# A routing matrix built in groups of four tokens: 36 blocks of the first expert table computed between the groups, and the weighted one-hots handed to GpSimd

## The chip, the core and the metric

The kernel runs on one core of a Trainium2 chip. Its engines are TensorE (PE in the profile; its weight loads are PEld), VectorE (DVE), ScalarE (ACT), GpSimd (POOL) and SyncE (SP), which here only issues DMAs. The metric is the device time of one execution in microseconds (us), as the median of several runs. Before the change it is 1849.74 us (three runs, 1848.17 to 1851.37 us).

## What is computed

The reference is a two-layer chain on 256 tokens of width 1024. The change touches one part of it, the PEER layer (product keys into a table of 16384 experts):

```python
q = (t @ w_q).reshape(n_tok, PEER_HEADS, 2, PEER_HALF)
sc = jnp.einsum("thpk,hpnk->thpn", q, sub_keys)
s_top, i_top = lax.top_k(sc, 16)                    # per head and half
...                                                 # 16 x 16 sums, best 16 of them
idx = i_top[..., 0] * 128 + i_top[..., 1]           # expert = (i, j)
g = jax.nn.softmax(best, axis=-1)
act = gelu(einsum("phkd,pd->phk", u_tab[idx], t))
out = einsum("phk,phkd->pd", g * act, v_tab[idx])
```

The kernel does not gather experts. It computes every expert for every token: block j of `u_tab` holds the 128 experts (i, j), so `gelu(u_block_j @ t)` is a tile of 128 experts by 256 tokens. It is multiplied by the routing matrix W[i, j, token], which is zero but where the token chose the expert, and the product is multiplied by block j of `v_tab`. There are 128 blocks in each table, 512 KB each.

## The kernel before

Work on fp32 operands goes in two forms. In the first, a 128 x 1024 piece of weights is loaded to a slot of a ring of four (`raw`), ACT copies it to fp32r (`high`, `take_high`), and DVE makes the rest (`low` = raw - high, `take_low`); TensorE then takes three products of the halves. `project_in` (L944 to L946) is 8 x 3 matmuls with 256 columns and makes a block of u; `project_out` (L963 to L967) is 12 matmuls with 512 columns and adds a block of v to banks 0 to 3. In the second form ("native", L1028) the fp32 operands are used as they are.

The PEER layer has four stages, one behind the other.

1. Selection. In four rounds TensorE makes queries and scores, DVE takes the top sixteen of each (the longest chain here), and TensorE fills its time with 24 native blocks of u (`EARLY_OF_ROUND` = 4, 4, 4, 12), the last 24 blocks of the table. ACT leaves their gelu in `arena`, where the routing matrix will lie.
2. TensorE computes block 0 of u, turns the selected weights, i and j to tokens-in-columns (`sel_turned`, L1039), ACT copies them to `chosen`, TensorE computes blocks 1 and 2.
3. The routing matrix, 64 groups of four tokens. For each token one matmul of two 128 x 128 one-hot tiles gives W[:, :, token] (L1054): the one-hot of i (DVE, one 128 x 512 instruction for the group, L1563), and the one-hot of j times the weight. The latter is made by DVE for 2.5 of four tokens (L1567) and by ACT for 1.5 (two instructions each, L735 and L743). ACT copies columns 0 to 103 to `arena` (L754), DVE multiplies the last 24 into the gelus that lie there (L1557). No blocks are computed, and no DMA runs, because a ring slot holds `chosen` and SP waits in `expert_step(0)` until all one-hots are there.
4. The expert loop, 128 steps. Step j is `project_out` of block j of v and, as long as j + 3 < LATE = 104, `project_in` of block j + 3 of u. Steps 0 to 100 have both, 101 to 127 have only v.

GpSimd takes some inverse roots of variances (`tensor_tensor` with pow on a 128 x 1 tile, L551) and is idle otherwise. The order on each engine is as written, and an engine works through its instructions in that order, held by semaphores. In stage 3 a group has two sets of one-hot tiles in turn (`n % 2`): a new one waits for `scat_done` of the group two back.

Of the kernel before, what the change touches and what calls it, by code (L numbers as in the profile page):

```python
# [44 lines left out]
PARTS = 128  # L45
# [23 lines left out]
EARLY = sum(EARLY_OF_ROUND)  # L69
LATE = NKEYS - EARLY  # L70

# [38 lines left out]
STREAM = [("mix", 8 * KC), ("mix_out", KC), ("query", 16), ("expert", NKEYS + LATE),  # L110
# [50 lines left out]

def piece_u(j, it=0):

    return Piece("expert", j if j < 3 else 2 * j - 2, it, 8)
# [21 lines left out]
def build(nc, x, w_mix, w_gate, w_out, w_query, keys, u_tab, v_tab, diff_qk, diff_v, diff_out,  # L186
# [3 lines left out]
    with ctx:  # L190
# [17 lines left out]
        ffn_params = sb("ffn_params", [PARTS, 2 * FF_CHUNKS * 4])  # L208
        subln = sb("subln", [PARTS, PARTS])
        stats = sb("stats", [PARTS, 64])  # L210
# [20 lines left out]
        def weights_of(token, j, j_end):  # L231

            return arena[:, :].rearrange("p (j t) -> p j t", t=SEQ)[:, j:j_end, bass.ds(token, 4)].rearrange("p j t -> p t j")
# [5 lines left out]
        def act_tokens(g):  # L239

            return (3,) if g % 2 == 0 else (2, 3)

        def scattered(g):

            return bank(g).rearrange("p (t j) -> p t j", t=4)
# [16 lines left out]
        chosen = raw[:, 2 * D:2 * D + 3 * SEQ]  # L262
        minus_weight = raw[:, 2 * D + 3 * SEQ:3 * D]
        distance = [ps[:, 7 * HALF + PARTS * n:7 * HALF + PARTS * (n + 1)] for n in range(4)]
# [96 lines left out]
        one_hots_ready, act_one_hots_ready = sem("one_hots_ready"), sem("act_one_hots_ready")  # L361
        distance_ready, scat_done, w_written = sem("distance_ready"), sem("scat_done"), sem("w_written")
# [82 lines left out]
        def _(sp):  # L445
# [21 lines left out]
            sp.dma_start(ffn_params[:, :], ffn_params_in).then_inc(ffn_params_loaded, 16)  # L467
# [5 lines left out]
            for it, early in enumerate(EARLY_OF_ROUND):  # L473
                for q in range(4 * it, 4 * it + 4):
                    load(Piece("query", q), w_query[q])
                if it == 3:
                    for j in range(3):
                        load(piece_u(j), u_tab[j])
                if it == 0:

                    sp.wait_ge(merged_ready, KC)
                for p in range(p, p + early):
                    if p >= 4:
                        sp.wait_ge(early_done, p - 3)
                    sp.dma_start(early_u[p % 4], u_tab[LATE + p]).then_inc(early_loaded[p % 4], 16)
                p += 1
                if it == 0:

                    sp.wait_ge(h_ready, TB)
                    sp.dma_start(h_saved, h_tok[:, :]).then_inc(h_kept, 16)  # L490
            def expert_step(j, it):
                if j == NKEYS - 2:

                    sp.wait_ge(coef_low, LATE)
# [7 lines left out]
                if opening(it) and j == 0:  # L502

                    sp.wait_ge(one_hots_ready, SEQ // 4)
                    sp.wait_ge(act_one_hots_ready, SEQ // 4)
# [37 lines left out]
        def _(pool):  # L543
# [10 lines left out]
            inverse_roots(0, 3)  # L554
# [13 lines left out]
        def _(a):  # L568
# [49 lines left out]
            a.activation(stats[:, 60:61], stats[:, 61:62], ACT.Square)  # L618
# [77 lines left out]
            for it in range(4):  # L696
                for q in range(4):
# [5 lines left out]
                    if 4 * it + q < 15:  # L703
                        ahead(p)
# [7 lines left out]
                for early in range(early, early + EARLY_OF_ROUND[it]):  # L712
                    if early == EARLY - 4:

                        a.wait_ge(shifted_ready, 1)
                        a.activation(sel[:, 0:SEQ], sel[:, 0:SEQ], ACT.Exp).then_inc(exp_ready, 1)
                    a.wait_ge(early_done, early + 1)
                    a.activation(part((LATE + early) * SEQ, SEQ), bank(4 + early % 4, 0, SEQ), ACT.Gelu_apprx_tanh
                                 ).then_inc(early_gelu, 1)
                early += 1  # L720
            v0, u0 = piece_v(0), piece_u(0)
            take_high(v0)
            ahead(u0)
            for b in range(2):
                a.wait_ge(sel_turned, b + 1)
                n = (2 - b) * SEQ
                a.activation(chosen[:, b * HALF:b * HALF + n], bank(b, 0, n), ACT.Copy).then_inc(chosen_ready, 1)

            a.activation(minus_weight, bank(0, 0, SEQ), ACT.Copy, scale=-1.0).then_inc(chosen_ready, 1)
            a.wait_ge(chosen_ready, 3)  # L730

            def distances(token, g):

                for u in act_tokens(g):
                    ins = a.activation(distance[2 * (g % 2) + u - 2], iota, ACT.Abs, scale=-1.0,  # L735
                                       bias=at(chosen, token + (2 * SEQ + u), 1))
                ins.then_inc(distance_ready, 1)

            def act_one_hots(token, g, n):

                a.wait_ge(distance_ready, n)
                for u in act_tokens(g):
                    ins = a.activation(one_hot_w[g % 2][:, u * PARTS:(u + 1) * PARTS], distance[2 * (g % 2) + u - 2], ACT.Relu,  # L743
                                       scale=at(minus_weight, token + u, 1), bias=at(chosen, token + u, 1))
                ins.then_inc(act_one_hots_ready, 1)

            def scatter_round(it, last=False):
                for g in range(4):  # L750
                    if not (last and g >= 2):
                        distances(it * 16 + (4 * g + 8), g)
                    a.wait_ge(scat_done, it * 4 + (g + 1))
                    a.activation(weights_of(it * 16 + 4 * g, 0, LATE), scattered(g)[:, :, 0:LATE], ACT.Copy).then_inc(w_written, 1)  # L754
                    if not (last and g >= 2):
                        act_one_hots(it * 16 + (4 * g + 8), g, it * 4 + (g + 3))

            a.wait_ge(h_kept, 16)
            for g in range(2):
                distances(4 * g, g)  # L760
                act_one_hots(4 * g, g, g + 1)
            with a.Fori(0, SEQ // 16 - 1) as it:
                scatter_round(it)
            scatter_round(SEQ // 16 - 1, last=True)


# [28 lines left out]
            a.wait_ge(scat_done, SEQ // 4)  # L795
            gelu_block(0, first=True)
            gelu_block(1, first=True)
# [131 lines left out]
        def _(pe):  # L929
# [103 lines left out]

            pe.wait_ge(early_gelu, EARLY)
            project_in(piece_u(0), bank(4, 0, SEQ))
# [7 lines left out]
            for j in (1, 2):  # L1043
                project_in(piece_u(j), bank(4 + j, 0, SEQ))


            def scatter_round(it):
                for g in range(4):
                    pe.wait_ge(one_hots_ready, it * 4 + (g + 1))
                    pe.wait_ge(act_one_hots_ready, it * 4 + (g + 1))  # L1050
                    if not opening(it):
                        pe.wait_ge(early_weighed, it * 4 + (g - 3))
                    for u in range(4):
                        ins = pe.matmul(bank(g, u * PARTS, PARTS), one_hot[g % 2][:, u * PARTS:(u + 1) * PARTS],  # L1054
                                        one_hot_w[g % 2][:, u * PARTS:(u + 1) * PARTS], start=True, stop=True)
                    ins.then_inc(scat_done, 1)

# [861 lines left out]
```

## Time and profile before

| | |
|---|---|
| median of 3 runs | 1849.74 us |
| profiled execution: its span (the page gives no other time of it) | 1851.6 us |
| stage 3, from the first to the last group | about 374.6 to 477.1 us |
| expert loop, from the first matmul of v | from 479.74 us |
| busy: PE, DVE, ACT, POOL | 93%, 68%, 50%, 1% |

The span is from the first to the last instruction. A busy PE is not PE at its peak, since matmuls are pipelined and their ends are modelled: the distance from one start to the next says what one costs. The same holds for ACT and DVE where rows overlap.

### The profile page before, as it was taken

Reading aid. Unit: us, or ns where it says so; the run is one execution under the profiler, and the core shown is the slowest. Engines: PE = TensorE matmul, PEld = TensorE weight load, DVE = VectorE, ACT = ScalarE, POOL = GpSimd, SP = SyncE. Lnnn points to the kernel's source line nnn. Section 1 sums busy time; section 2 is a strip of 40 time slices with the busy share of each in tenths; the row PEclk is TensorE's granted clock in tenths of the full one; section 3 lists DMA queues with packets and bytes.
Section 4 is the critical chain, followed back from the end, with each engine's and each line's share of the span. In section 5 each row is a group of like instructions: output and inputs, shape, how many; then the busy total and the mean of one; then the engine's idle time right before and its main releaser. Section 6 shows DMA issues by size and latency. Waiting matters only on the chain.

```text
span 1851.6 us, 32033 instructions
## 1 busy us (share of the span) xinstructions
PE 1724.4 (93%) x11238; PEld 1567.2 (85%) x11238; DVE 1260.4 (68%) x2341; ACT 925.5 (50%) x1554; POOL 21.9 (1%) x29
## 2 busy tenths in 40 slices
PE   7999799977899999999999998886999989989997
PEld 7999699865799999999999886765999968779997
DVE  6888689999655555555555565685767675566766
ACT  5666533299644444444444454544444444544443
POOL 0000000000000000000000000001000000000000
PEclk9999899999999999999999998998999989999999
DMA  6556634300455555555555565322555544245552
GB/s 198 174 189 201 204 119 144 114 0 0 149 191 182 191 183 190 183 188 186 189 185 187 187 219 175 115 93 90 193 183 191 182 137 126 80 137 186 188 182 102
DMA packets 81305, 292.19 MB, mean 158 GB/s; under 512 B 9056, under 2 KB 10848, under 8 KB 80864
## 3 DMA queue, kind: packets, MB, share of 16 engines
q1 hardware_dynamic: 79632, 286.00, 45.9%
q10 hardware_dynamic: 1616, 5.45, 0.9%
q8 instruction: 34, 0.56, 0.1%
q14 instruction: 23, 0.19, 0.0%
HBM read 289.31 MB, written 2.10 MB: 157 GB/s over the span
## 4 chain that ended last, share of the span: by engine, by line
PE 75%; DVE 10%; issue 9%; ACT 5%; ACTq 1%; POOL 0%; DMA 0%; SPq 0%; DVEq 0%; POOLq 0%
PE ps L944 14%; PE ps L946 14%; PE ps L945 14%; PE ps L963 10%; PE ps L965 10%; PE ps L967 10%; DVE low L1230 1%; ACT h_tok L743 1%; ACT ps L735 1%; ACT arena L754 1%; PE ps L1102 1%; PE ps L939 1%; DVE arena L1529 1%; DVE arena L1531 1%; DVE h_tok L1297 1%
## 5 line engine op out<-in xcount | busy, mean ns | idle before, releaser
L1230 DVE TENSOR_TENSOR low<-raw,high 128x1024 fp32r<-128x1024 f32 (+1 forms) x517 | 623.1, 1211 | 438.8 <-ACT high L595 425.6
L595 ACT ACTIVATE high<-raw 128x1024 fp32r<-128x1024 f32 (+1 forms) x517 | 540.9, 1049 | 621.8 <-PE ps L946 335.5
L944 PE MATMUL ps<-xh,low 128*128 128x256 f32 x2376 | 680.8, 287 | 13.7 <-DVE xl L1251 7.6
L945 PE MATMUL ps<-xl,high 128*128 128x256 f32 x2376 | 675.1, 284 | 0.0
L946 PE MATMUL ps<-xh,high 128*128 128x256 f32 x2376 | 675.0, 284 | 0.0
L944 PEld LDWEIGHTS ps<-xh,low 128*128 128x128 f32 x2376 | 458.7, 193 | 24.4 <-DVE xl L1251 8.2
L945 PEld LDWEIGHTS ps<-xl,high 128*128 128x128 f32 x2376 | 458.7, 193 | 7.4 <-issue 1.7
L946 PEld LDWEIGHTS ps<-xh,high 128*128 128x128 f32 x2376 | 458.3, 193 | 0.0
L963 PE MATMUL ps<-high,yl 128*128 128x512 f32 x688 | 215.2, 394 | 2.8 <-issue 2.6
L965 PE MATMUL ps<-low,yh 128*128 128x512 f32 x688 | 213.8, 392 | 0.0
L967 PE MATMUL ps<-high,yh 128*128 128x512 f32 x688 | 213.3, 391 | 0.0
L965 PEld LDWEIGHTS ps<-low,yh 128*128 128x128 f32 x688 | 129.8, 189 | 28.7
L967 PEld LDWEIGHTS ps<-high,yh 128*128 128x128 f32 x688 | 129.7, 189 | 28.2
L963 PEld LDWEIGHTS ps<-high,yl 128*128 128x128 f32 x688 | 120.3, 190 | 20.0 <-issue 2.8
L1054 PE MATMUL ps<-h_tok 128*128 128x128 f32 x512 | 73.1, 286 | 29.6 <-DVE h_tok L1567 17.0
L1054 PEld LDWEIGHTS ps<-h_tok 128*128 128x128 f32 x512 | 61.9, 191 | 40.7 <-issue 14.6
L1028 PE MATMUL ps<-arena 128*128 128x256 f32 x384 | 83.5, 379 | 0.0
L1028 PEld LDWEIGHTS ps<-arena 128*128 128x128 f32 x384 | 72.7, 190 | 9.7
L754 ACT ACTIVATE arena<-ps 128x416 f32 (+1 forms) x64 | 71.8, 1122 | 3.7 <-PE ps L1054 3.7
L963 PE MATMUL ps<-high,xl 128*128 128x512 f32 x160 | 53.3, 416 | 9.5 <-DVE xl L1240 4.2
L743 ACT ACTIVATE h_tok<-ps,raw 128x128 f32<-128x128 f32 x96 | 53.3, 668 | 0.1
L965 PE MATMUL ps<-low,xh 128*128 128x512 f32 x160 | 51.7, 405 | 0.0
(215 smaller groups left out, 1479.4 us busy)
## 6 DMA issues: line engine op xcount, KB each, us to landing
raw<-in_v_tab SPq DMA_DIRECT2D x128, 512.0 KB, 3.3
raw<-in_u_tab SPq DMA_DIRECT2D x104, 512.0 KB, 3.2
raw<-in_ffn_in SPq DMA_DIRECT2D x88, 512.0 KB, 3.2
raw<-in_w_mix SPq DMA_DIRECT2D x56, 512.0 KB, 4.4
raw<-in_ffn_out SPq DMA_DIRECT2D x44, 512.0 KB, 3.3
arena<-in_u_tab SPq DMA_DIRECT2D x24, 512.0 KB, 3.4
raw<-in_w_query SPq DMA_DIRECT2D x16, 512.0 KB, 5.8
raw<-in_diff_qk SPq DMA_DIRECT2D x16, 512.0 KB, 3.4
```

The source lines that it names most:

```text
L595: a.activation(cols(high, p, 0, n), cols(raw, p, 0, n), ACT.Copy).then_inc(slot_high[p.slot], 1)
L743: ins = a.activation(one_hot_w[g % 2][:, u * PARTS:(u + 1) * PARTS], distance[2 * (g % 2) + u - 2], ACT.Relu, scale=at(minus_weight, token ...
L754: a.activation(weights_of(it * 16 + 4 * g, 0, LATE), scattered(g)[:, :, 0:LATE], ACT.Copy).then_inc(w_written, 1)
L944: pe.matmul(dst, left[1], right[0], start=start, stop=False)
L945: pe.matmul(dst, left[0], right[1], start=False, stop=False)
L946: return pe.matmul(dst, left[0], right[0], start=False, stop=stop)
L963: pe.matmul(bank(2 * t + half), src_low[:, xs], cols(high, p, half * HALF, HALF), start=first, stop=False)
L965: pe.matmul(bank(2 * t + half), src_high[:, xs], cols(low, p, half * HALF, HALF), start=False, stop=False)
L967: ins = pe.matmul(bank(2 * t + half), src_high[:, xs], cols(high, p, half * HALF, HALF), start=False, stop=last)
L1028: ins = pe.matmul(bank(4 + early % 4, 0, SEQ), early_u[early % 4][:, k * PARTS:(k + 1) * PARTS], chunk_of(xf, k), start=(k == 0), stop=(k ...
L1054: ins = pe.matmul(bank(g, u * PARTS, PARTS), one_hot[g % 2][:, u * PARTS:(u + 1) * PARTS], one_hot_w[g % 2][:, u * PARTS:(u + 1) * PARTS], ...
L1230: v.tensor_tensor(cols(low, p, 0, n), cols(raw, p, 0, n), cols(high, p, 0, n).bitcast(F32), ALU.subtract).then_inc(slot_low[p.slot], 1)
```

## The change

- Of the 104 blocks of u that came behind the selection, 36 are now "staged": blocks 103 down to 68 (`staged_block(k)` = 103 - k). Four (LEAD) are computed after the native ones, before the selection is turned. The other 32 stand between the groups of the routing matrix, one behind each second group, in PSUM banks 4 to 7 in turn. LATE falls from 104 to 68.
- A staged block that is computed behind group n holds tokens of which the weights are already known. ACT writes the gelu of those in place in PSUM, and DVE multiplies them into `arena`; the gelu of the other tokens goes to `arena`, and is weighed by the group's own multiplication, which grows from 24 columns to 28 and then by one for each second group, up to 59. ACT's copy shrinks by the same.
- The one-hot of j times the weight is made by GpSimd for all tokens, one `tensor_scalar` (is_equal, mult) on 128 x 128 each, 256 in all. DVE's 160 and ACT's 2 x 96 instructions for it are gone.
- Weights, i and j move from the ring slot to `spare` and `yh`, so the ring goes on through stage 3 and SP's wait is gone. Blocks 0, 1 and 2 of u are computed behind the last group. ACT's exp of the scores moves from the middle of the last native blocks to behind them. The loops over groups are written out.

```diff
+LEAD, STAGED = 4, 36
+FIRST_NATIVE = NKEYS - NATIVE
+EARLY = NATIVE + STAGED
 LATE = NKEYS - EARLY
+def first_staged(n):
+    return FIRST_NATIVE - LEAD - n // 2
...
+        weight = spare[:, :]
+        sel_i, sel_j = (yh[:, SEQ * n:SEQ * n + SEQ].bitcast(F32) for n in range(2))
...  (GpSimd)
+            pool.wait_ge(chosen_ready, 3)
+            pool.wait_ge(h_kept, 16)
+            for n in range(GROUPS):
+                if n >= 2:
+                    pool.wait_ge(scat_done, n - 1)
+                for u in range(4):
+                    t = 4 * n + u
+                    ins = pool.tensor_scalar(one_hot_w[n % 2][:, u * PARTS:(u + 1) * PARTS], iota, sel_j[:, t:t + 1], weight[:, t:t + 1],
+                                             ALU.is_equal, ALU.mult)
+                ins.then_inc(j_hots_ready, 1)
...  (ScalarE)
+            for k in range(LEAD):
+                p = piece_staged(k)
+                a.wait_ge(slot_done[p.slot], p.count)
+                a.activation(staged_part(k, 0, SEQ), staged_bank(k, 0, SEQ), ACT.Gelu_apprx_tanh).then_inc(staged_ready, 1)
+                ahead(p)
+            a.wait_ge(sel_turned, 1)
+            a.activation(yh[:, 0:SEQ], bank(0, SEQ, SEQ), ACT.Copy).then_inc(chosen_ready, 1)
...
+            for n in range(GROUPS):
+                a.wait_ge(scat_done, n + 1)
+                j_end = first_staged(n)
+                a.activation(weights_of(n, 0, j_end), scattered(n)[:, :, 0:j_end], ACT.Copy).then_inc(w_written, 1)
+                if n % 2 == 1:
+                    k, t = LEAD + n // 2, 4 * (n + 1)
+                    p = piece_staged(k)
+                    if n > 1:
+                        ahead(p.later(-1))
+                    a.wait_ge(slot_done[p.slot], p.count)
+                    ins = a.activation(staged_bank(k, 0, t), staged_bank(k, 0, t), ACT.Gelu_apprx_tanh)
+                    if t < SEQ:
+                        ins = a.activation(staged_part(k, t, SEQ), staged_bank(k, t, SEQ), ACT.Gelu_apprx_tanh)
+                    ins.then_inc(staged_ready, 1)
...  (TensorE)
-            project_in(piece_u(0), bank(4, 0, SEQ))
+            for k in range(LEAD):
+                project_in(piece_staged(k), bank(4 + k % 4, 0, SEQ))
...
+            for n in range(GROUPS):
+                pe.wait_ge(i_hots_ready, n + 1)
+                pe.wait_ge(j_hots_ready, n + 1)
+                if n >= 4:
+                    pe.wait_ge(early_weighed, n - 3)
+                for u in range(4):
+                    ins = pe.matmul(bank(n % 4, u * PARTS, PARTS), one_hot[n % 2][:, u * PARTS:(u + 1) * PARTS],
+                                    one_hot_w[n % 2][:, u * PARTS:(u + 1) * PARTS], start=True, stop=True)
+                ins.then_inc(scat_done, 1)
+                if n % 2 == 1:
+                    k = LEAD + n // 2
+                    pe.wait_ge(staged_ready, LEAD)
+                    if k >= 2 * LEAD:
+                        pe.wait_ge(staged_weighed, k - 2 * LEAD + 1)
+                    project_in(piece_staged(k), bank(4 + k % 4, 0, SEQ))
+            for j in range(3):
+                pe.wait_ge(staged_weighed, STAGED - LEAD - 3 + j)
                 project_in(piece_u(j), bank(4 + j, 0, SEQ))
...  (VectorE)
-                for q in range(4 * it, min(4 * it + 4, 15)):
+                for q in range(4 * it, 4 * it + 4):
                     ahead(Piece("query", q))
...
+            for n in range(0, GROUPS, 2):
+                k = LEAD + n // 2
+                if n + 2 < GROUPS:
+                    v.wait_ge(scat_done, n + 1)
+                    i_hots(n + 2)
+                if n >= 2:
+                    weigh_staged(k - 1)
+                if n + 3 < GROUPS:
+                    v.wait_ge(scat_done, n + 2)
+                    i_hots(n + 3)
+                weigh_group(n)
+                weigh_group(n + 1)
+                take_low(piece_staged(k).later(1))
```

On TensorE, the start of the routing matrix before: the turns are L1039, block 1 and 2 of u stand between them and the first group, and the groups (L1054, four matmuls each) stand back to back.

```order
L1039 MATMUL ps<-consts,arena 128x128 [waits sel_ready]
L1039 MATMUL ps<-consts,arena 128x128 x5
...
L1054 MATMUL ps<-h_tok 128x128 [waits act_one_hots_ready,one_hots_ready]
L1054 MATMUL ps<-h_tok 128x128 x3
L1054 MATMUL ps<-h_tok 128x128 [waits act_one_hots_ready,one_hots_ready]
```

The same place now (turns L1058, groups L1069, `project_in` L962 to L964):

```order
L1058 MATMUL ps<-consts,arena 128x128 x5
L1069 MATMUL ps<-h_tok 128x128 [waits j_hots_ready,i_hots_ready]
L1069 MATMUL ps<-h_tok 128x128 x3
L1069 MATMUL ps<-h_tok 128x128 [waits j_hots_ready,i_hots_ready]
L1069 MATMUL ps<-h_tok 128x128 x3
...
L964 MATMUL ps<-xh,high 128x256
L1069 MATMUL ps<-h_tok 128x128 [waits j_hots_ready,i_hots_ready]
```

Behind each second group stand the 24 matmuls of a block. Four blocks stand ahead of the turns, where there was one, and none between the turns and the first group.

On VectorE, two groups before (L1563 the one-hots of i, L1567 those of j with the weight, L1557 the multiplication of the native blocks):

```order
L1563 TENSOR_TENSOR h_tok<-raw,consts 128x512 [waits scat_done]
L1567 TENSOR_SCALAR h_tok<-consts,raw 128x128 x3
L1557 TENSOR_TENSOR arena<-arena,ps 128x4x24 [waits w_written]
L1563 TENSOR_TENSOR h_tok<-raw,consts 128x512 [waits scat_done]
L1567 TENSOR_SCALAR h_tok<-consts,raw 128x128 x2
L1557 TENSOR_TENSOR arena<-arena,ps 128x4x24 [waits w_written]
```

And two groups now (L1578 the one-hots of i, L1592 a staged block's known tokens, L1586 the multiplication of the groups, L1255 the low half of a piece of the ring):

```order
L1578 TENSOR_TENSOR h_tok<-yh,consts 128x512 [waits scat_done]
L1592 TENSOR_TENSOR arena<-arena,ps 128x8 [waits staged_ready]
L1578 TENSOR_TENSOR h_tok<-yh,consts 128x512 [waits scat_done]
L1586 TENSOR_TENSOR arena<-arena,ps 128x4x29 [waits w_written] x2
L1255 TENSOR_TENSOR low<-raw,high 128x1024 [waits slot_high2]
```

The five `tensor_scalar` are gone; a low half of 1024 columns and the staged multiplication are new. On GpSimd, the first two groups and the third:

```order
L577 TENSOR_TENSOR stats<-stats 128x1 [waits var_ready] x3
L589 TENSOR_SCALAR h_tok<-consts,yh,spare 128x128 [waits h_kept,chosen_ready]
L589 TENSOR_SCALAR h_tok<-consts,yh,spare 128x128 x7
L589 TENSOR_SCALAR h_tok<-consts,yh,spare 128x128 [waits scat_done]
L589 TENSOR_SCALAR h_tok<-consts,yh,spare 128x128 x3
```

Before, nothing stood here but the inverse roots. Every group's four instructions now wait for the group two back.

## Rows read from the trace of the kernel before

**Rows 1.** The page: busy time of the engines.
```profile
PE 1724.4 (93%) x11238; PEld 1567.2 (85%) x11238; DVE 1260.4 (68%) x2341; ACT 925.5 (50%) x1554; POOL 21.9 (1%) x29
```

**Rows 2.** Busy time by stretch; the first row names the columns.
```profile
core 0: us, PE busy (x) PEld busy (x) DVE busy (x) ACT busy (x) POOL busy (x), PEclk, DMA share, GB/s
374.40:477.20 102.80, 73.14 (x514) 61.83 (x513) 96.96 (x280) 101.07 (x249) 0.00 (x0) 1.00 0.00 0
479.70:485.00 5.30, 5.26 (x13) 4.13 (x14) 3.06 (x4) 2.38 (x3) 0.00 (x0) 0.50 0.99 342
500.00:1050.00 550.00, 550.00 (x3525) 501.96 (x3524) 305.76 (x392) 263.86 (x392) 0.00 (x0) 1.00 0.55 187
1057.00:1115.00 58.00, 58.00 (x257) 48.04 (x256) 34.79 (x44) 29.15 (x43) 0.00 (x0) 1.00 0.62 216
```

**Rows 3.** Timeline of stage 3: start us, us, engine, line, operation, xcount [idle before].
```profile
402.90 0.97 PEld L1054 LDWEIGHTS ps<-h_tok 128*128 128x128 f32 x8 [0.33 <-issue]
402.92 0.69 DVE L1563 TENSOR_TENSOR h_tok<-raw,consts 128x512 f32<-128x512 f32 x1
403.52 0.60 DVE L1567 TENSOR_SCALAR h_tok<-consts,raw 128x128 f32<-128x128 f32 x2
404.19 0.34 DVE L1557 TENSOR_TENSOR arena<-arena,ps 128x96 f32 x1
404.56 1.14 ACT L754 ACTIVATE arena<-ps 128x416 f32 x1
405.23 0.69 ACT L743 ACTIVATE h_tok<-ps,raw 128x128 f32<-128x128 f32 x1
```

**Rows 4.** Timeline of the expert loop's start and of its middle.
```profile
479.74 1.19 PE L963 MATMUL ps<-high,yl 128*128 128x512 f32 x2 [2.62 <-issue]
484.99 0.41 PE L944 MATMUL ps<-xh,low 128*128 128x256 f32 x1
...
1042.03 1.06 ACT L595 ACTIVATE high<-raw 128x1024 fp32r<-128x1024 f32 x1 [1.48 <-PE ps L967]
1045.87 0.37 ACT L772 ACTIVATE h_tok<-ps 128x256 f32<-128x256 f32 x1
```

**Rows 5.** The chain in order of time: start us, us, what.
```profile
303.74 4.54 DVE low L1230 x4
335.84 3.40 DVE low L1230 x3
368.00 0.88 PE ps L1039 x6
374.62 0.91 PE ps L1054 x8
```

**Rows 6.** Timeline: TensorE's first block of u.
```profile
361.55 0.39 PE L944 MATMUL ps<-xh,low 128*128 128x256 f32 x1 [0.47 <-ACT arena L718]
361.77 0.28 PE L945 MATMUL ps<-xl,high 128*128 128x256 f32 x1
361.89 0.28 PE L946 MATMUL ps<-xh,high 128*128 128x256 f32 x1
```

**Rows 7.** Timelines: GpSimd, alone and beside VectorE.
```profile
0.24 0.10 POOL L1910 MEMSET const-float32-0.0<- 128x1 f32 x1 [0.24 <-issue]
0.28 0.10 POOL L1910 MEMSET const-float32-1.0<- 128x1 f32 x1
...
1126.73 0.55 POOL L551 TENSOR_TENSOR stats<-stats 128x1 f32<-128x1 f32 x1 [909.56 <-DVE stats L1271]
...
1288.11 1.28 DVE L1306 SCALAR_TENSOR_TENSOR arena<-h_tok,stats,arena 128x1024 f32<-128x1024 f32 x1
```

**Rows 8.** The chain again, at the same place.
```profile
1288.28 1.54 POOL stats L551
```

**Rows 9.** Groups on GpSimd: us busy, mean ns of one.
```profile
L563 POOL MEMSET arena<- 128x4096 f32 x1 | 3.5, 3505 | 0.0
L556 POOL MEMSET arena<- 128x256 f32 x1 | 0.3, 310 | 0.0
```

More of the change, by code:

```diff
@@ L476, in _ @@
                 if it == 3:
-                    for j in range(3):
-                        load(piece_u(j), u_tab[j])
+                    for k in range(LEAD):
+                        load(piece_staged(k), u_tab[staged_block(k)])
                 if it == 0:
@@ L490, in _ @@
                     sp.dma_start(h_saved, h_tok[:, :]).then_inc(h_kept, 16)
+            for k in range(LEAD, STAGED):
+                load(piece_staged(k), u_tab[staged_block(k)])
+            for j in range(3):
+                load(piece_u(j), u_tab[j])
             def expert_step(j, it):
                 if j == NKEYS - 2:
+                    sp.wait_ge(j_hots_ready, GROUPS)
+                    sp.dma_start(ffn_params, ffn_params_in).then_inc(ffn_params_loaded, 16)
                     sp.wait_ge(coef_low, LATE)
@@ L730, in _ @@
[L730 to L745, printed above, removed]
@@ L749, in scatter_round @@
[L749 to L756, printed above, removed]
@@ L758, in _ @@
[L758 to L764, printed above, removed]
+            a.wait_ge(shifted_ready, 1)
+            a.activation(sel[:, 0:SEQ], sel[:, 0:SEQ], ACT.Exp).then_inc(exp_ready, 1)
+            for k in range(LEAD):
+                p = piece_staged(k)
+                a.wait_ge(slot_done[p.slot], p.count)
+                a.activation(staged_part(k, 0, SEQ), staged_bank(k, 0, SEQ), ACT.Gelu_apprx_tanh).then_inc(staged_ready, 1)
+                ahead(p)
@@ L767, in gelu_block @@
+            ahead(piece_staged(STAGED - 1))
             def gelu_block(j, it=0, first=False):
@@ L1042, in _ @@
                     ins.then_inc(sel_turned, 1)
-            for j in (1, 2):
-                project_in(piece_u(j), bank(4 + j, 0, SEQ))
[L1047 to L1056, printed above, removed]
-            rounds(pe, SEQ // 16, scatter_round)
+            for n in range(GROUPS):
[13 more added lines that the diff above has]
+                    project_in(piece_staged(k), bank(4 + k % 4, 0, SEQ))
+            for j in range(3):
+                pe.wait_ge(staged_weighed, STAGED - LEAD - 3 + j)
+                project_in(piece_u(j), bank(4 + j, 0, SEQ))
             def expert_step(j, it):
@@ L1065, in expert_step @@
                 if j + 3 < LATE:
-                    if not (opening(it) and j == 0):
+                    if opening(it) and j == 0:
+                        pe.wait_ge(staged_weighed, STAGED - LEAD)
+                    else:
                         pe.wait_ge(gelu_ready, it * 4 + j)
@@ L1602, in _ @@
             coef_low_part(0)
+            ahead(piece_u(0))
             coef_low_part(1)
```

117 lines of the change are left out of this document (53 added, 64 removed).

## The prediction

> **What bounds the kernel now.** I read the page first, then the stretches, then the timeline inside the one that stands out. The page has TensorE at 93% busy [rows 1], but that is a mean over stages. Cut into stretches, the expert loop has it busy 550.00 of 550 us, and the routing matrix (374.4 to 477.2 us) 73.14 of 102.80 us, while ACT is busy 101.07 and DVE 96.96 there, GpSimd 0 and the DMA engines 0 [rows 2]. So that one stage of 103 us is bound by ACT and DVE with TensorE waiting, and the 650 us behind it by TensorE alone. What the change can gain is in that hole: TensorE work of the second stretch put into the first.
>
> The size of a moved block comes from two stretches at full granted clock. With both projections, 3525 matmuls in 550 us at 36 a step are 97.9 steps of 5.62 us; with v only, 257 in 58 us at 12 a step are 21.4 steps of 2.71 us [rows 2]. A block of u therefore costs 2.90 us of the loop, and its 24 matmuls at 0.12 us from start to start are the same 2.88 [rows 6]. In both forms TensorE is the bound, so the loop gets shorter by the whole of it: **36 x 2.90 = 104.4 us**. The 36 more steps with v alone stay at 2.71, as the rows of today's 27 show, and they load 216 GB/s against 187, which is shown to hold [rows 2].
>
> **What the interval ahead of the loop costs now.** I measure it from the first block of u on TensorE (361.55, behind the native blocks) to the first block of v (479.74) [rows 4, 6]: 118.2 us. That first v block starts behind 2.62 us without a matmul, and its 12 matmuls take 479.74 to 484.99 = 5.25 us at a granted clock of 0.50 (1.2 GHz), against 2.71: 2.5 us more, and 0.4 for the next few [rows 2, 4]. Sum 121.1 us. After the change TensorE goes from the last group through blocks 0 to 2 right into v, so this start at the low level goes; if it doesn't, 2.9 us come back.
>
> **What it costs after.**
> - Ahead of the groups: four blocks, 4 x 2.88 = 11.5, to 373.1 us; six turns, 0.9 [rows 5], to 374.0. DVE now takes four low halves in the last round where it took three (4.54 against 3.40 us [rows 5]), so the selection ends 1.1 us later, near 369; the blocks hide that. ACT's exp moves behind the native blocks, ahead of 363 by its place, and is also hidden. But ACT does the fourth gelu and a high half (1.06 [rows 4]) before it copies the turned data (three copies of 256 columns at 0.37 [rows 4]): to 375.7. Then DVE makes two one-hots of i (0.60 each, start to start [rows 3]) and GpSimd four tiles. First group near 377.8: 16.3 us from 361.55, of which 3.8 are a wait of TensorE.
> - The groups: 32 pairs of T each, a pair being two groups and one block.
> - Behind them: blocks 0 to 2, 8.6 us, which stood ahead of it before. DVE's last low halves and the first coefficients lie beside them (some 4 us), so v starts without a gap.
>
> Change = 16.3 + 32 T + 8.6 - 121.1 - 104.4 = **32 T - 200.6 us**. It is zero at T = 6.27 us; one pair is 3.2 us now.
>
> **What sets T.** TensorE: two groups at 0.97 (eight weight loads, which follow each other at that [rows 3]) and 2.88: **4.82 us**. ACT: two copies, 0.67 each from start to start for 416 columns and less for 400 to 276 [rows 3], a high half 1.06, the gelu of 256 columns in two pieces, some 0.6 by 0.37 for one [rows 4]: 3.0. Its 192 one-hot instructions, which filled it, are gone. DVE: two one-hots 1.20, one low half 1.14 (a quarter of 4.54 [rows 5]), two multiplications from 0.34 for 96 columns [rows 3] to about 0.5 for 236, the staged one 0.3: 3.5. Walked through a pair, neither is late: DVE's low half ends about 1.2 us before TensorE wants the next group. DMA is one load in a pair, half of what the loop carries.
>
> GpSimd is the term that no row shows: eight `tensor_scalar` on 128 x 128 in a pair, p each. A new pair may start 1.1 us into the present one (the group two back is done) and must be ready 4.7 us later, so up to p = 0.59 it would be hidden if it had its port to itself. From below: a memset takes (3505 - 310)/3840 = 0.83 ns a column [rows 9], 0.107 us for 128, and small ones follow each other in 0.035 us [rows 7]: p = 0.14. From above: the one-column pow takes 0.55 us with reading, arithmetic and writing [rows 7]; with 127 more columns at the memset's rate 0.66. I take the middle, p = 0.40. It could also be slower per column than a memset; that is past my upper row.
>
> It does not have the port to itself. At 1288.28 a pow that takes 0.55 us elsewhere took 1.54 us: VectorE was in an instruction with two SBUF operands from 1288.11 to 1289.39, and the pow ended 0.44 us behind that [rows 7, 8]. So GpSimd stood still for the whole of it. In a pair DVE has three such instructions, the two one-hots of i (from `yh` and `consts`) and the low half (from `raw` and `high`): 1.20 + 1.14 = 2.34 us. The one-hots are released by the same group as GpSimd's tiles and so always meet them. The multiplications have one operand in PSUM; I count them as free. Hence T = 8 x 0.40 + 2.34 = **5.54 us**, GpSimd as the bound, TensorE waiting 0.7 us in each pair.
>
> The Trainium skill ("SBUF — State Buffer", Who interferes with whom) says that a VectorE instruction with two SBUF inputs contends with a GpSimd one that reads SBUF, as an exclusive lock held for the whole instruction. By that rule the trace agrees: 1.54 us against 0.55. Without the rule GpSimd would need 3.2 us, TensorE would set T = 4.82, and the sum would be 46 us faster.
>
> **The sum.** 32 x 5.54 - 200.6 = 177.3 - 200.6 = -23.3 us. The span profiled is 1851.6 us, 0.1% above the median of 1849.7; I take the difference from the median: **1826.4 us**.
>
> **Rivals.**
> - B, TensorE is the bound. If p is 0.3 or less, or the waits for the port overlap with what GpSimd does before it reads, T = 4.82 to 5.0 and the change is 154.2 - 200.6 = -46.4: **1803.3 us**. For it: the memset row, and that a lock is only between 8 short instructions. Against: the 1.54 us.
> - C, GpSimd turns it slower. It decides from T = 6.27, or p = 0.49 with the lock, in the 64 groups. The price is 2.56 us for each 0.01 us of p: at 0.55, between break-even and my upper row, T = 6.74 and +15.1: **1865 us**. For it: the pow row, of which most isn't arithmetic of 128 columns. Against: memsets in a row follow each other far faster than their own length. Nothing else queues behind GpSimd's tiles but the groups, so all of the excess is TensorE's wait, and it would idle a third of the stage.
> - D, the gain is eaten evenly: p within 0.477 to 0.506, **1850 us**.
>
> The skill ("GPSIMD Engine Reference", 4.1 Engine selection) calls GpSimd about line rate for one input and advises VectorE for elementwise work; line rate would be an estimate of 0.11 us of arithmetic for 128 columns. No row here has such an instruction. By that page p would be near my lower bound, which speaks for B.
>
> **How the numbers follow.** My forecast (p from 0.30 to 0.475, T 4.9 to 6.1, 1805 to 1846 us) has a chance of 0.42, B 0.28, C 0.25, D 0.05. A measurement of this kernel tells about 0.2% (3.7 us) from no change. Faster: 0.42 + 0.28 = 0.70; within: 0.05; slower: 0.25. The range goes from 1801, just under B, to 1864, which leaves out about half of C: some 0.15 in all.
>
> **What would show it.** The start-to-start distance of the GpSimd rows (0.40 forecast), and their length where a DVE one-hot or low half runs beside them, shows p and the lock. The distance of every second group (5.54) shows T, and the waits what ends TensorE's idle time before a group: GpSimd in my case and in C, nothing in B, DVE's low half if I mis-sized it. The expert loop must be 104 us shorter at 5.62 and 2.71 us a step; a v-only step above 2.8 would say that loads, not TensorE, bound it. Granted clock 1.00 at the first v block shows the 2.9 us. The forecast is wrong if T is bound by ACT or DVE, or if the stage stalls between staged blocks on a bank.

## The result, and the profile after

The changed kernel takes **1897.53 us** (median of 4, 1895.95 to 1898.83) against 1849.97 before: ratio 1.0252, 95% interval 1.0235 to 1.0268. It is 47.6 us slower, where 23.3 us faster was forecast. The profiled spans are 1897.0 and 1851.6 us, 45.4 apart.

Busy time by stretch, kernel after (columns as in [rows 2]); the stretches are the routing matrix with the staged blocks, the loop with both projections, and the loop with v only:

```profile
380.00:620.00 240.00, 179.12 (x1248) 172.62 (x1248) 114.42 (x187) 88.16 (x155) 239.45 (x253) 0.87 0.21 69
640.00:1000.00 360.00, 360.00 (x2307) 328.56 (x2306) 199.75 (x256) 172.91 (x257) 0.00 (x0) 1.00 0.58 187
1010.00:1160.00 150.00, 150.00 (x663) 124.20 (x663) 91.18 (x111) 75.28 (x110) 0.00 (x0) 1.00 0.62 203
```

The first row answers to the one of 374.4 to 477.2 in [rows 2]. There ACT and DVE were full and GpSimd idle; now GpSimd is busy 239.45 of 240 us and everything else waits. A row of GpSimd counts as busy while its instruction is held up, so this time holds the waits for the port too. A pair of groups and its block are 40 records of matmuls, so 1248 are 31.2 pairs of 7.7 us. The loop rows are as before: 36 records a step make 5.62 us, 12 a step 2.71.

The chain in order of time, kernel after, around one pair (start us, us, what):

```profile
474.71 0.43 issue
475.15 1.14 PE ps L1069 x8
476.32 0.70 DVE h_tok L1578
477.02 1.53 issue
478.55 2.04 PE ps L1069 x8
480.59 0.21 PE ps L962
```

The 1.53 us of "issue" are time in which TensorE waits for GpSimd's fourth tile: the semaphore's giver is not shown. The timeline of GpSimd (L589) and DVE in the same pair shows what it does:

```profile
475.81 0.79 POOL L589 TENSOR_SCALAR h_tok<-consts,yh,spare 128x128 f32<-128x128 f32 x1
476.32 0.69 DVE L1578 TENSOR_TENSOR h_tok<-yh,consts 128x512 f32<-128x512 f32 x1 [1.77 <-PE ps L1069]
476.58 1.09 POOL L589 TENSOR_SCALAR h_tok<-consts,yh,spare 128x128 f32<-128x128 f32 x1
477.66 0.79 POOL L589 TENSOR_SCALAR h_tok<-consts,yh,spare 128x128 f32<-128x128 f32 x1
481.97 1.83 POOL L589 TENSOR_SCALAR h_tok<-consts,yh,spare 128x128 f32<-128x128 f32 x1
482.07 1.22 DVE L1255 TENSOR_TENSOR low<-raw,high 128x1024 fp32r<-128x1024 f32 x1
483.79 0.79 POOL L589 TENSOR_SCALAR h_tok<-consts,yh,spare 128x128 f32<-128x128 f32 x1
```

A tile that meets nothing takes 0.79 us and the next starts 0.77 behind it. The one-hot of i begins when a tile is 0.51 us under way: that tile keeps its 0.79, and the one behind it takes 0.30 more. The low half (1.22 us) begins when a tile is only 0.10 us under way, and that tile itself takes 1.04 more.

In these rows DVE loses nothing, but it does in others. Two cases from the same trace, each a tile and the DVE instruction that begins 0.18 and 0.14 us into it:

```profile
505.24 0.78 POOL L589 TENSOR_SCALAR h_tok<-consts,yh,spare 128x128 f32<-128x128 f32 x1
505.42 1.33 DVE L1255 TENSOR_TENSOR low<-raw,high 128x1024 fp32r<-128x1024 f32 x1
581.62 0.79 POOL L589 TENSOR_SCALAR h_tok<-consts,yh,spare 128x128 f32<-128x128 f32 x1
581.76 0.84 DVE L1578 TENSOR_TENSOR h_tok<-yh,consts 128x512 f32<-128x512 f32 x1 [2.34 <-PE ps L1069]
```

Here the tile keeps its time and the DVE instruction is 0.11 and 0.15 us longer than its usual 1.22 and 0.69. Of 59 one-hots of i between 385 and 612 us 14 took 0.72 to 0.84 us, of 30 low halves five took 1.27 to 1.33; before, all of the one-hots took 0.68 or 0.69 and the low halves 1.22 or 1.23. So each side can hold up the other, and GpSimd loses far more.

Where the interval ahead of the loop went, in single rows of the timeline of TensorE (L962 the first staged block, L1069 the first group, L981 the first block of v):

```profile
362.40 0.39 PE L962 MATMUL ps<-xh,low 128*128 128x256 f32 x1 [0.47 <-ACT arena L751]
380.29 2.05 PE L1069 MATMUL ps<-h_tok 128*128 128x128 f32 x8 [5.45 <-POOL h_tok L589]
634.10 0.63 PE L981 MATMUL ps<-high,yl 128*128 128x512 f32 x2
```

From 362.40 to 380.29 are 17.9 us (16.3 in the sum). From 380.29 to 634.10 are 253.8 us = 32 T + 8.6, so T = 7.66 us (7.69 by the count above, which leaves out both ends). From the first block of v to the end of the span are 1262.94 us, where the kernel before has 1371.86: 108.9 shorter, against 107.3 in the sum (104.4 and 2.9). The first block of v runs at its full speed (0.63 for two matmuls, where [rows 4] have 1.19).

### The profile page after: what moved, and what is told of

The parts are those of the page before. It is cut to its first block, busy times and chain, and to the rows that moved or that the text cites. A ratio compares the mean times of both kernels' runs of the same rounds, so it can differ in the third digit from the quotient of the medians.

```text
span 1897.0 us, 30957 instructions
## 1 busy us (share of the span) xinstructions
PE 1739.9 (92%) x11238; PEld 1589.2 (84%) x11238; DVE 1229.4 (65%) x2177; ACT 869.3 (46%) x1393; POOL 264.9 (14%) x285
## 3 DMA queue, kind: packets, MB, share of 16 engines
q1 hardware_dynamic: 79632, 286.00, 46.1%
## 4 chain that ended last, share of the span: by engine, by line
PE 84%; issue 9%; DVE 4%; ACT 1%; POOL 1%; DMA 0%; DVEq 0%; ACTq 0%; POOLq 0%
PE ps L962 15%; PE ps L963 15%; PE ps L964 15%; PE ps L981 10%; PE ps L983 9%; PE ps L985 9%; PE ps L1046 4%; PE ps L1069 4%; DVE h_tok L1578 1%; POOL h_tok L589 1%; PE ps L957 1%; PE ps L1127 1%; DVE h_tok L1322 1%; ACT high L633 1%; DVE low L1255 0%
## 5 line engine op out<-in xcount | busy, mean ns | idle before, releaser
L1255 DVE TENSOR_TENSOR low<-raw,high 128x1024 fp32r<-128x1024 f32 (+1 forms) x517 | 622.9, 1211 | 361.0 <-ACT high L633 347.0
L962 PE MATMUL ps<-xh,low 128*128 128x256 f32 x2376 | 693.7, 292 | 12.9 <-DVE xl L1276 6.8
L963 PE MATMUL ps<-xl,high 128*128 128x256 f32 x2376 | 684.6, 288 | 0.0
L964 PE MATMUL ps<-xh,high 128*128 128x256 f32 x2376 | 684.0, 288 | 0.0
L962 PEld LDWEIGHTS ps<-xh,low 128*128 128x128 f32 x2376 | 469.4, 198 | 22.3 <-DVE xl L1276 7.6
L963 PEld LDWEIGHTS ps<-xl,high 128*128 128x128 f32 x2376 | 468.8, 197 | 5.9 <-issue 1.7
L964 PEld LDWEIGHTS ps<-xh,high 128*128 128x128 f32 x2376 | 468.2, 197 | 0.0
L589 POOL TENSOR_SCALAR h_tok<-consts,yh,spare 128x128 f32<-128x128 f32 x256 | 243.0, 962 | 159.4 <-ACT yh L767 158.9
L981 PE MATMUL ps<-high,yl 128*128 128x512 f32 x688 | 213.7, 392 | 0.1
L577 POOL TENSOR_TENSOR stats<-stats 128x1 f32<-128x1 f32 x14 | 12.3, 889 | 1337.9 <-DVE stats L1296 1337.9
L1069 PE MATMUL ps<-h_tok 128*128 128x128 f32 x512 | 78.5, 302 | 66.2 <-issue 49.5
L981 PEld LDWEIGHTS ps<-high,yl 128*128 128x128 f32 x688 | 122.1, 189 | 19.8 <-DVE yl L1265 1.0
L1069 PEld LDWEIGHTS ps<-h_tok 128*128 128x128 f32 x512 | 69.2, 210 | 72.9 <-issue 61.2
L1578 DVE TENSOR_TENSOR h_tok<-yh,consts 128x512 f32<-128x512 f32 x64 | 45.2, 707 | 130.6 <-PE ps L1069 125.7
L772 ACT ACTIVATE arena<-ps 128x400 f32<-128x400 f32 (+31 forms) x64 | 49.3, 770 | 101.6 <-PE ps L1069 101.6
L1046 PEld LDWEIGHTS ps<-arena 128*128 128x128 f32 x384 | 72.7, 190 | 9.7
```

Source lines behind the costliest of these rows:

```text
L589: ins = pool.tensor_scalar(one_hot_w[n % 2][:, u * PARTS:(u + 1) * PARTS], iota, sel_j[:, t:t + 1], weight[:, t:t + 1], ALU.is_equal, ALU. ...
L962: pe.matmul(dst, left[1], right[0], start=start, stop=False)
L963: pe.matmul(dst, left[0], right[1], start=False, stop=False)
L964: return pe.matmul(dst, left[0], right[0], start=False, stop=stop)
L981: pe.matmul(bank(2 * t + half), src_low[:, xs], cols(high, p, half * HALF, HALF), start=first, stop=False)
L1046: ins = pe.matmul(bank(4 + early % 4, 0, SEQ), early_u[early % 4][:, k * PARTS:(k + 1) * PARTS], chunk_of(xf, k), start=(k == 0), stop=(k ...
```

## The experiments

Three theories. **G**: GpSimd's own time for a tile, 0.77 us, sets the pair, and the port that it shares with VectorE adds to it. **S**: the staged order itself stalls TensorE (banks, gelus, waits). **L** (experiments 3, 4 and 6): the port is the greater part, and VectorE's `tensor_scalar` adds to it. "The stage" is the stretch from the first group to the first block of v. Pairs counted in a window leave out the ends of the stage, where a pair can be longer or shorter.

**1. Staged order without GpSimd.** VectorE makes three of four weighted tiles, ScalarE one, in two instructions each as in the kernel before, with what lies between the two kept in the buffer `yl`. GpSimd's loop over the groups is gone. The split is 3 to 1, where the kernel before had 2.5 to 1.5.

```diff
+DVE_OF, ACT_OF, POOL_OF = (((0, 1, 2), (0, 1, 2)), ((3,), (3,)), ((), ()))
...  (VectorE)
-                                iota4, ALU.is_equal).then_inc(i_hots_ready, 1)
+                                iota4, ALU.is_equal)
+                for u in DVE_OF[n % 2]:
+                    ins = v.tensor_scalar(one_hot_w[n % 2][...], iota, sel_j[...], weight[...], ALU.is_equal, ALU.mult)
+                ins.then_inc(i_hots_ready, 1)
...  (ScalarE)
+                if n + 2 < GROUPS:
+                    distances(n + 2)
                 a.wait_ge(scat_done, n + 1)
+                if n + 2 < GROUPS:
+                    act_one_hots(n + 2)
```

> The staged order of the changed kernel, with the weighted one-hots made by VectorE (three of four tokens) and ScalarE (one of four, two instructions each) as in the kernel before; GpSimd makes none. Theory G (GpSimd's own time per tile, about 0.77 us from start to start in the changed kernel, sets the pair at 7.6 us): the pair is now set by VectorE, 3.3 us of its other work and six tiles of 0.30, 5.1 to 5.4 us; the time is about 1815 to 1825 us, 25 to 35 below the kernel before. Rival S (the staged order itself stalls TensorE, by its waits on banks and gelus): the pair stays above 7 us and the time above 1875 us.

Measured 1810.13 us, ratio 0.9788 (0.9771 to 0.9804): 39 us faster than before, 87 faster than the change with GpSimd. The stretch:

```profile
380.00:530.00 150.00, 146.63 (x1217) 143.64 (x1217) 149.15 (x364) 123.65 (x274) 0.00 (x0) 1.00 0.34 103
```

1217 records are 30.4 pairs of 4.93 us, and DVE is the full engine (149.15 of 150). G had put the pair at 5.1 to 5.4 us and the time at 1815 to 1825, both a little too high; S had it above 7 us and 1875. S falls: the staged order is worth 39 us by itself.

**2. GpSimd alone, no staging.** The kernel before, with all weighted tiles by GpSimd. VectorE's and ScalarE's instructions for them are gone.

```diff
...  (GpSimd)
-            inverse_roots(0, 3)
+            inverse_roots(0, 2)
+            for n in range(SEQ // 4):
+                if n >= 2:
+                    pool.wait_ge(scat_done, n - 1)
+                for u in range(4):
+                    ins = pool.tensor_scalar(one_hot_w[n % 2][...], iota, chosen[...], chosen[...], ALU.is_equal, ALU.mult)
+                ins.then_inc(act_one_hots_ready, 1)
```

> The kernel before with one thing changed: all weighted one-hots by GpSimd; no block is staged. Theory G: a pair of groups is eight tiles of 0.77 and some 0.6 for VectorE's two one-hots of i, 6.8 us in place of 3.2, so 32 x 3.6 = 115 us more: about 1965 us. Rival S: GpSimd is not the bound, the stage stays within 20 us of what it was, about 1850 to 1870 us.

Measured 1969.03 us, ratio 1.0657 (1.0639 to 1.0675): 120 us slower. GpSimd is busy 210 of 210 us:

```profile
380.00:590.00 210.00, 122.03 (x476) 105.34 (x477) 64.41 (x119) 52.38 (x60) 210.00 (x240) 0.51 0.00 0
```

476 records of 8 a group are 59.5 groups of 3.53 us, 7.06 a pair (6.8 expected), against 3.20 in [rows 2]. So the two halves of the change have opposite signs: -39 and +120. Together they are +48, not +81, because the time GpSimd needs is then partly filled by the staged blocks.

**3. Half of the tiles by GpSimd.**

```diff
...  (VectorE)
+                for u in (0, 1):
+                    ins = v.tensor_scalar(...)
...  (GpSimd)
-                for u in range(4):
+                for u in (2, 3):
                     ins = pool.tensor_scalar(...)
```

> The changed kernel with two of four weighted one-hots made by VectorE, two by GpSimd. Theory G: GpSimd needs 4 x 0.77 and a lock share, 4.5 us in a pair, VectorE 4.5, TensorE 4.8: the pair is 4.9 to 5.3 us, the time about 1805 to 1820 us. Rival L (the port lock between VectorE and GpSimd is the cost, and VectorE's tensor_scalar adds to it): the pair is above 6 us, the time above 1840 us.

Measured 1819.41 us, ratio 0.9842 (0.9825 to 0.9858); 1218 records in 160 us are 5.25 us a pair. At the upper end of what G says (to 5.3 us and 1820). But the 128 tiles now take 1224 ns in the mean, and GpSimd is still nearly full:

```profile
380.00:540.00 160.00, 148.58 (x1218) 144.71 (x1217) 139.89 (x306) 87.02 (x152) 149.62 (x123) 0.99 0.32 100
```

Four tiles alone would be 3.1 us in a pair of 5.25. The other part is VectorE's work beside them. Which of it, the timelines of both engines in one group tell (L1579 the one-hot of i, L1583 VectorE's tiles, L1591 the multiplications, L590 GpSimd's tiles):

```profile
452.39 0.69 DVE L1579 TENSOR_TENSOR h_tok<-yh,consts 128x512 f32<-128x512 f32 x1
452.46 1.39 POOL L590 TENSOR_SCALAR h_tok<-consts,yh,spare 128x128 f32<-128x128 f32 x1
453.00 0.60 DVE L1583 TENSOR_SCALAR h_tok<-consts,yh,spare 128x128 f32<-128x128 f32 x2
453.52 1.00 DVE L1591 TENSOR_TENSOR arena<-arena,ps 128x168 f32<-128x168 f32 x2
453.83 0.80 POOL L590 TENSOR_SCALAR h_tok<-consts,yh,spare 128x128 f32<-128x128 f32 x1
```

The tile that meets the one-hot of i takes 1.39 us; in the changed kernel, with no `tensor_scalar` of VectorE behind the one-hot, a tile that begins 0.08 us behind it takes 1.28. So the two `tensor_scalar` cost it 0.1 us at most, and the multiplications, with one operand in PSUM, cost the next tile nothing. With two tiles in a group, more of GpSimd's tiles lie beside an instruction with two SBUF operands, and that raises the mean.

**4. Three engines.** VectorE two tiles, ScalarE one, GpSimd one.

The code is that of experiment 1 with GpSimd's loop kept for its tile.

```diff
+DVE_OF, ACT_OF, POOL_OF = (((0, 1), (0, 1)), ((3,), (3,)), ((2,), (2,)))
...  (GpSimd)
-                for u in range(4):
+                for u in POOL_OF[n % 2]:
```

> The changed kernel with the weighted one-hots shared by three engines: two of four tokens by VectorE, one by ScalarE, one by GpSimd. Theory G: no engine needs more than TensorE's 4.8 us in a pair (VectorE 4.5, ScalarE 4.3, GpSimd 1.6 and its lock share), the pair is 4.85 to 5.0 us and the time about 1803 to 1812 us. Rival L: above 5.5 us a pair, 1825 us or more.

Measured **1803.60 us**, ratio 0.9752 (0.9736 to 0.9769): 45.6 us faster than the kernel before, 94 faster than the changed one, the best of all. TensorE is full:

```profile
380.00:520.00 140.00, 140.00 (x1202) 139.89 (x1201) 135.00 (x298) 121.05 (x271) 81.80 (x61) 1.00 0.36 111
```

1202 records are 30.05 pairs of 4.66 us (4.85 to 5.0 expected). In this window TensorE is never without work, so other engines have nothing left to give there. No run has two tiles on VectorE and two on ScalarE, so it is not shown that GpSimd's one tile is needed for this.

**5. The forms of a GpSimd instruction.** In the changed kernel, ahead of the groups, seven runs of up to eight instructions each, the last one a repeat of the first. `probe(n, f)` issues them on n columns.

```diff
...  (GpSimd)
+            probe(128, lambda o, i: pool.tensor_scalar(o, i, one, two, ALU.is_equal, ALU.mult))
+            probe(32, ...)                                            # the same on 32 columns
+            probe(256, ...)                                           # on 256
+            probe(128, lambda o, i: pool.tensor_scalar(o, i, one, None, ALU.is_equal))
+            probe(128, lambda o, i: pool.tensor_scalar(o, i, 3.0, 0.5, ALU.is_equal, ALU.mult))
+            probe(128, lambda o, i: pool.tensor_tensor(o, i, iota, ALU.mult))
...
```

> The changed kernel with 60 extra GpSimd instructions ahead of the routing matrix, where GpSimd is idle: the tile's own form (tensor_scalar is_equal, mult, two per-partition operands) on 128, 32 and 256 columns, then on 128 columns with one operation, with two immediate operands, and a tensor_tensor. Read by the distance from start to start. Theory F (most of 0.77 us is fixed per instruction): 32 columns take 0.6 us or more and 256 below 1.0. Theory C (the columns are the cost, 5 to 6 ns each): 32 columns about 0.2 to 0.3, 256 about 1.45 us. If the per-partition operands are the cost, the form with immediates is clearly shorter.

The timeline (start us, us from the first start to the last end, count). Its windows leave out the instructions that lay beside a VectorE instruction with two SBUF operands (one each at L599, L600 and L602), one more behind it at L600 and L602, and the repeat:

```profile
227.32 6.25 POOL L597 TENSOR_SCALAR h_tok<-consts,stats 128x128 f32<-128x128 f32 x8 [9.73 <-DVE arena L1494]
233.68 3.63 POOL L598 TENSOR_SCALAR h_tok<-consts,stats 128x32 f32<-128x32 f32 x8
237.40 3.63 POOL L599 TENSOR_SCALAR h_tok<-consts,stats 128x256 f32<-128x256 f32 x3
246.08 3.50 POOL L600 TENSOR_SCALAR h_tok<-consts,stats 128x128 f32<-128x128 f32 x6
249.66 4.91 POOL L601 TENSOR_SCALAR h_tok<-consts 128x128 f32<-128x128 f32 x8
256.77 2.56 POOL L602 TENSOR_TENSOR h_tok<-consts 128x128 f32<-128x128 f32 x6
```

With one instruction's length taken off and divided by the rest: 0.78 us for 128 columns, 0.45 for 32, 1.20 for 256. The three widths lie close to one line, of 0.34 us at no columns and 3.4 ns a column; taken as the fixed part, the 0.34 is an estimate. Neither F nor C of this expectation is right alone: of 0.78, 0.34 is fixed and 0.43 is columns. One operation takes 0.58, two with immediate operands 0.61, a `tensor_tensor` product 0.42. The second operation costs 0.20 us, the per-partition operands 0.17. This execution took 1896.36 us.

Two of the instructions left out show the port at work: the fourth on 256 columns lay beside four low halves, the first `tensor_tensor` beside a VectorE `tensor_tensor` of 1.20 us.

```profile
241.01 3.62 POOL L599 TENSOR_SCALAR h_tok<-consts,stats 128x256 f32<-128x256 f32 x1
254.66 1.73 POOL L602 TENSOR_TENSOR h_tok<-consts 128x128 f32<-128x128 f32 x1
259.44 5.51 POOL L603 TENSOR_SCALAR h_tok<-consts,stats 128x128 f32<-128x128 f32 x7
```

They took 3.62 us where 1.22 is usual and 1.73 where 0.45 is. The third row is the repeat of the first form. Its instructions lie, but for the seventh, beside VectorE instructions that read one SBUF tile (`MAX8` and its kin), and they keep the pace of 0.78.

**6. Little use of the port.** VectorE's one-hots of i and its low halves between the groups on 8 columns. The other columns are left out, so this kernel doesn't compute the layer.

```diff
-                v.tensor_tensor(one_hot[n % 2].rearrange("p (t i) -> p t i", t=4), ...)
+                v.tensor_tensor(one_hot[n % 2][:, 0:8], sel_i[...], iota[:, 0:8], ALU.is_equal)
...
-                take_low(piece_staged(k).later(1))
+                v.tensor_tensor(cols(low, q, 0, 8), cols(raw, q, 0, 8), cols(high, q, 0, 8).bitcast(F32), ALU.subtract)
```

> The changed kernel in which VectorE's one-hots of i and the low halves of the pieces between the groups work on 8 columns only (the rest of these tiles keeps old data: that part of the computation is left out), so that VectorE hardly uses two SBUF operands in the stage. Theory G with the lock as a smaller part: a pair falls from 7.6 to 8 x 0.773 = 6.2 us, and the time to about 1852 us. If the lock were the greater part, the pair would fall to 5 us; if there is no lock, it stays at 7.6 us and 1895 us.

One execution: 1857.73 us, beside 1852.44 of the kernel before. The tiles follow each other at one pace, eight to a pair, in GpSimd's timeline of this kernel:

```profile
449.84 6.24 POOL L589 TENSOR_SCALAR h_tok<-consts,yh,spare 128x128 f32<-128x128 f32 x8
```

And its busy time between the first groups and the loop:

```profile
385.00:575.00 190.00, 151.18 (x1226) 146.50 (x1226) 51.53 (x184) 85.72 (x151) 188.63 (x244) 0.99 0.26 84
```

1226 records are 30.65 pairs of 6.20 us, which is the tiles' own time (8 x 0.775). Against 7.66 the port's share is 1.46 us a pair. Measured over the whole stage it is a little less: 209.7 us (380.21 to 589.90) against 253.8 are 44.1 us, 1.38 a pair, and the kernel's time is 39.8 us shorter in this one execution, 5 us above G's 1852. So the port costs the changed kernel 40 to 47 us. That is the smaller part, as G had it; L as the main cause falls.

**7. Tiles by one operation.** The routing matrix without weights, which leaves part of the layer out.

```diff
-                    ins = pool.tensor_scalar(one_hot_w[...], iota, sel_j[:, t:t + 1], weight[:, t:t + 1], ALU.is_equal, ALU.mult)
+                    ins = pool.tensor_scalar(one_hot_w[...], iota, sel_j[:, t:t + 1], None, ALU.is_equal)
```

> The changed kernel with GpSimd's tiles made by one operation (is_equal) in place of two: the weight is left out of the routing matrix. In the run of the forms such an instruction took 0.58 us from start to start against 0.776. If a pair is eight tiles plus a port share of about 1.4 us whatever the form, it falls from 7.6 to 8 x 0.58 + 1.4 = 6.0 us and the time by 32 x 1.6 = 51 us to about 1845 us. If the instructions' length is a result of the waits and not a cause, the pair stays above 7 us.

One execution: 1849.71 us, beside 1851.26 before (median of 7).

```profile
385.00:565.00 180.00, 143.95 (x1177) 139.12 (x1177) 109.79 (x177) 84.18 (x148) 179.93 (x237) 1.00 0.29 89
```

1177 records are 29.4 pairs of 6.12 us, 0.1 above the sum of 8 x 0.58 and 1.4; 1845 us were expected. The length of the instruction is a cause: 0.2 us less in each tile took 1.5 us from a pair and 48 us from the kernel.

**8. A quarter by GpSimd, three quarters by VectorE.** As in 3, with `(0, 1, 2)` and `(3,)`.

> The changed kernel with three of four weighted one-hots made by VectorE and one by GpSimd; ScalarE makes none. By the sums: VectorE 3.3 + 6 x 0.30 = 5.1 us in a pair, GpSimd 1.5 and its port share, TensorE 4.66. Theory G with VectorE as the next bound: a pair of 5.0 to 5.2 us, the time 1808 to 1818 us, like the run without GpSimd, so that the gain of the three-engine version is ScalarE's share and not GpSimd's. Rival: any bit of GpSimd work costs by the port, and the time is above 1825 us; or it frees VectorE as well as ScalarE did, and the time is 1803 us.

Measured 1811.25 us, ratio 0.9783 (0.9760 to 0.9806), the same as without GpSimd (1810.13, experiment 1). G had said 1808 to 1818.

```profile
380.00:530.00 150.00, 146.58 (x1219) 143.48 (x1218) 149.44 (x364) 87.02 (x152) 104.15 (x62) 1.00 0.33 104
```

VectorE is full at 4.92 us a pair. So one tile in four on GpSimd neither hurts nor helps while VectorE has three. Version 4 is 7.6 us faster than this one and 6.5 faster than version 1: there VectorE has two, and TensorE is the full engine.

## Why the prediction was wrong

The sum was 32 T - 200.6 us. With the measured T of 7.66 it gives +44.5, with 1.6 us more ahead of the first group +46.1; the spans differ by 45.4. So the frame held, and the fault lies in T.

- **The step that failed** is the term of GpSimd, "Hence T = 8 x 0.40 + 2.34". A tile takes 0.775 us from start to start, not 0.40: 8 x 0.375 = 3.0 us a pair, 96 us in all. Experiments 6 and 7 show that this time is the cause: with little use of the port the pair is still 6.20 us, and 0.2 us less in each tile takes 1.5 us from it. My upper row gave 0.66, so even the far end was too low, and my own break-even of 0.49 was passed by far. The rows behind it were wrong guides: I took the memset's 0.83 ns as the price of a column, where `tensor_scalar` has 3.4 ns [rows 9, experiment 5]. A memset has no input and no arithmetic. One row of the kernel before spoke against 0.66 as a far end, a pow on two columns:

```profile
1193.05 0.70 POOL L560 TENSOR_TENSOR stats<-stats 128x2 f32<-128x2 f32 x1 [64.44 <-DVE stats L1694]
```

It takes 0.15 us more than on one column (0.55 [rows 7]), where the memset's rate adds 0.001. A pow is no compare, so this gives no price for the tile, but it shows that a column with arithmetic isn't a memset's column. Of rival C, which I priced at 1865 us with 0.25, the mechanism was right and its price too small.
- **The port.** The 2.34 us I charged are 1.46, or 1.38 over the whole stage (experiment 6 and the change): -28 to -31 us in all. That there is a lock, which [rows 7, 8] showed and the Trainium skill states ("SBUF — State Buffer", Who interferes with whom), is borne out: with short VectorE instructions the pair falls from 7.66 to 6.20. The page has the words "for the whole instruction" for VectorE's two-port modes; here a GpSimd instruction doesn't keep VectorE out for its whole length. In the changed kernel's timeline a tile that is 0.18 us or more under way when the VectorE instruction begins keeps its 0.79 us; one that is at most 0.12 us under way, or begins while that instruction runs, is held. So the part of a VectorE instruction that lies beside the rest of a running tile is free, and charging each in full was too much. The multiplications with one operand in PSUM, which I counted as free, are free (experiment 3). The two errors have opposite signs, and -28 hid part of +96: with p = 0.775 and 2.34 my own sum would have come out at +72.7. Without the port that sum stands at -46.4, which is 23 us below my -23.3; the "46 us faster" of the prediction is right only against the kernel before.
- **TensorE's bound.** I had 4.82 us; the full pair is 4.66 (experiment 4). A group was taken at 0.97, the time from the first weight load's start to the last one's end; the loads follow each other at 0.11 (16 loads of two groups in 1.79 us in experiment 4), so a group costs 0.89.
- **The loop.** Forecast 104.4 us shorter and 2.9 for the cold start of the first v block. The rows bear both out: steps of 5.62 and 2.71 us, the first v block at full clock, 108.9 us less from there to the end.
- **Ahead of the groups** 17.9 us against 16.3: the four tiles take 3.7 us, not 1.6. They start at 376.47, the first takes 1.35 us beside the two one-hots of i, the others 0.79.
- **VectorE and ScalarE** were not late, as forecast: in the changed kernel they are busy 3.67 and 2.83 us a pair (3.5 and 3.0 in the sum). Even with GpSimd's tiles on them the pair is 4.93 (experiment 1). The hole that [rows 2] showed was there: version 4 gains 45.6 us from it and ends at 1803.6 us. That this is rival B's number (1803.3) is in part luck, since B had T = 4.82. What took the gain away in the changed kernel is the choice of the engine.
- **The line rate** that the Trainium skill states ("GPSIMD Engine Reference", 4.1 Engine selection), cited for B: 128 columns take 0.43 us beyond the estimated fixed part in this form, not 0.11 (experiment 5). The measurement decides. The same section's advice, VectorE for elementwise work, is what the trace agrees with: VectorE's tile is 0.30 us [rows 3].

## What to carry to other kernels

Before work goes to an engine on which the trace has no row of that form, measure that form: the price of one instruction is multiplied here by 256, and the break-even was known (0.49 us). When a change has two parts, price each alone; here one was worth -39 us and the other +120. Spread over three engines, so that each stays under the bound of the fourth, the same tiles cost nothing; whether two of the three would do is open.

## What the runs showed of the hardware

- GpSimd, `tensor_scalar` with two operations and per-partition operands on fp32: 3.4 ns a column and, by the line through three widths, 0.34 us fixed (an estimate); 0.78 us for 128 columns, one operation 0.58, immediates 0.61; `tensor_tensor` product 0.42, less than `tensor_scalar` (experiment 5).
- GpSimd and VectorE instructions with two SBUF operands exclude each other for a part of their time, in both directions. A VectorE instruction that begins 0.14 to 0.26 us into a tile is longer by what is missing to about 0.29 us (0.84 in place of 0.69 at 0.14, 1.33 in place of 1.22 at 0.18), one that begins 0.30 to 0.65 us into it is not. So a tile seems to need the port only until about 0.3 us from its start; this is read from the rows and not tested by itself. GpSimd's tile takes up to 1.9 us in place of 0.79 beside a low half (changed kernel). In experiment 2 GpSimd lengthens VectorE's one-hots from 0.69 to 0.74 us in the mean:

```profile
L1568 DVE TENSOR_TENSOR h_tok<-raw,consts 128x512 f32<-128x512 f32 x58 | 43.1, 744 | 126.6 <-PE ps L1059 126.6
```

- VectorE instructions with one operand in PSUM, and those with one SBUF operand in experiment 5, leave GpSimd's tile at 0.78 to 0.80 us (experiments 3 and 5).
- TensorE's granted clock was 0.51 (1.2 GHz) all through stage 3 of experiment 2, where it waits between groups, and 0.87 in the mean in the changed kernel, where groups of 8 loads took 1.14 us or 2.04. Before, with shorter gaps, it was 1.00 [rows 2]. As GpSimd set the pace (busy 210.00 of 210 us and 239.45 of 240), this cost nothing here.
